# Weight units of a hybrid mixer and MoE kernel laid out so that each partition's 16 KB are contiguous in memory

## What is computed

```python
x_n = rms_norm(x, mix_norm_g); h = x_n @ w_in            # (1024, 9216)
a_val, a_gb, a_gc, h_glu, q, h_gate = split(h)
y_a = (a_gb * conv3(a_gc * a_val)) @ w_out_a
u   = silu(layer_norm(conv31(glu(h_glu + b_glu)) + conv_b_b)); y_b = u @ w_out_b + b_out_b
y_x = cross_attention(q, rms_norm(mem), w_kv) @ w_out_x   # 4 heads, 256 memory tokens
x   = x + (gate0 * y_a + gate1 * y_b + gate2 * y_x) @ w_o
z   = rms_norm(x, ffn_norm_g)                             # top-1 group of 4, top-2 of its 8 experts
for e in range(32):
    gate, up = split(z @ w_gate_up[e])                    # (1024, 1024)
    x += combine[:, e] * ((silu(gate) * up) @ w_down[e])  # (512, 1024)
return rms_norm(x, final_norm_g)
```

## Time and profile before

| what | value |
|---|---|
| median of 3 runs (lowest, highest) | 1006.33 us (1005.08, 1006.57) |
| profiled execution, own device time | not given on the page |
| profiled execution, span | 1004.3 us |
| data moved by DMA | 270.6 MB, mean 269 GB/s |
| packets of SyncE's queue | 116,688 |
| dense part, routing, expert loop | about 0 to 400, 400 to 440, 440 to 990 us |

### The profile page before, as it was taken

How to read it: one execution, slowest core, us unless ns; L and a number is a source line. 1 busy time by engine, 2 the same in 40 slices (tenths; PEclk the granted TensorE clock), 3 DMA queues, 4 the chain that set the end, 5 groups by cost and what they waited for, 6 DMA issues and landing times.

```text
span 1004.3 us, 17558 instructions
## 1 busy us (share of the span) xinstructions
PE 932.6 (93%) x6914; PEld 812.2 (81%) x6914; DVE 854.5 (85%) x812; ACT 668.9 (67%) x649; POOL 211.6 (21%) x178
## 2 busy tenths in 40 slices
PE   5999989899999999499999999999999999999996
PEld 5998989899899998377777777777777777777774
DVE  4369999998765666679999999999999999999996
ACT  5553434344544645468888888788888888888885
POOL 0149999960001100410000000000000000000000
PEclk9999999999999999799999999999999999999998
DMA  9944534355422595269999999999999999999931
GB/s 341 355 169 144 191 121 167 133 207 212 168 85 98 205 385 214 84 222 327 357 357 348 365 363 344 364 352 363 343 364 363 350 358 351 363 348 361 363 132 42
DMA packets 118592, 270.60 MB, mean 269 GB/s; under 512 B 3360, under 2 KB 5536, under 8 KB 118560
## 3 DMA queue, kind: packets, MB, share of 16 engines
q1 hardware_dynamic: 116688, 267.37, 73.5%
q10 hardware_dynamic: 1872, 2.79, 0.8%
HBM read 269.10 MB, written 1.05 MB: 269 GB/s over the span
## 4 chain that ended last, share of the span: by engine, by line
PE 54%; DVE 29%; ACT 9%; issue 5%; DMA 1%; ACTq 1%; POOL 0%; DVEq 0%; SPq 0%
PE ps L1342 18%; DVE lo L980 11%; PE ps L1167 6%; PE ps L1169 6%; PE ps L1168 6%; PE ps L1367 6%; ACT hi L637 5%; DVE conv L852 5%; PE ps L1331 5%; DVE lo_last L980 4%; DVE lo L765 4%; PE ps L1184 1%; PE ps L1183 1%; PE ps L1182 1%; ACT silu_sb L723 1%
## 5 line engine op out<-in xcount | busy, mean ns | idle before, releaser
L980 DVE TENSOR_TENSOR lo<-raw,hi 128x2048 fp32r<-128x2048 f32 x142 | 328.5, 2339 | 4.2 <-ACT hi L637 4.2
L637 ACT ACTIVATE hi<-raw 128x2048 fp32r<-128x2048 f32 x141 | 267.5, 1909 | 3.0 <-PE ps L1342 3.0
L765 DVE TENSOR_TENSOR lo<-raw,hi 128x2048 fp32r<-128x2048 f32 x62 | 149.0, 2405 | 32.0 <-ACT hi L450 30.7
L1167 PE MATMUL ps<-inA,hi 128*128 128x256 f32 x576 | 166.2, 288 | 9.5 <-DVE lo L765 8.4
L450 ACT ACTIVATE hi<-raw 128x2048 fp32r<-128x2048 f32 x63 | 120.4, 1913 | 75.6 <-PE ps L1169 48.9
L1169 PE MATMUL ps<-inA,lo 128*128 128x256 f32 x576 | 164.4, 285 | 0.0
L1168 PE MATMUL ps<-inA,hi 128*128 128x256 f32 x576 | 164.4, 285 | 0.0
L1342 PE MATMUL ps<-hi,xeT 128*128 128x512 f32 x384 | 154.6, 403 | 5.8 <-DVE lo L980 5.2
L1342 PE MATMUL ps<-lo,xeT 128*128 128x512 f32 x384 | 150.1, 391 | 0.0
L422 POOL TENSOR_TENSOR hT<-h_sb,hT 128x256 fp32r<-128x256 f32 x32 | 33.9, 1059 | 524.9 <-ACT hT L682 524.9
L1167 PEld LDWEIGHTS ps<-inA,hi 128*128 128x128 f32 x576 | 112.1, 195 | 11.8 <-DVE lo L765 11.8
(11 more groups left out here) (213 smaller groups left out, 1632.7 us busy)
## 6 DMA issues: line engine op xcount, KB each, us to landing
raw<-in_w_gate_up SPq DMA_DIRECT2D x64, 2048.0 KB, 7.8
raw<-in_w_down SPq DMA_DIRECT2D x32, 2048.0 KB, 7.8
raw<-in_w_in SPq DMA_DIRECT2D x17, 2048.0 KB, 8.1
raw<-in_w_kv SPq DMA_DIRECT2D x4, 2048.0 KB, 8.4
raw<-in_w_out_a SPq DMA_DIRECT2D x2, 2048.0 KB, 7.7
raw<-in_w_out_x SPq DMA_DIRECT2D x2, 2048.0 KB, 7.8
raw<-in_w_out_b SPq DMA_DIRECT2D x2, 2048.0 KB, 8.8
raw<-in_w_o SPq DMA_DIRECT2D x2, 2048.0 KB, 7.6
```

What stands on the lines that cost most here:

```text
L637: nc.scalar.activation(expert_half(hi, N0), raw_flat(slot, k % 2), ACT.Copy).then_inc(hi_made, 1)
L765: nc.vector.tensor_tensor(conv_half(lo, N), raw_half(slot, h, k_split), conv_half(hi, N).bitcast(f32), ALU.subtract).then_inc(lo_made, 1)
L980: nc.vector.tensor_tensor(expert_half(lo, N0), raw_flat(expert_slot(m), k % 2), expert_half(hi, N0).bitcast(f32), ALU.subtract).then_inc(l ...
L1167: mm(dst, w_hi[:, k, c * P:(c + 1) * P], acts[:, 0, k, :], start=(k == 0), stop=False)
```

## The change

The host builds two new arrays. `w_dense` holds the 30 dense units one after the other, `w_experts` gate, up and down of each expert; in both a unit is stored as 128 rows of 4,096 floats, row p being exactly what partition p of the slot holds. Loads keep their order, their slots, their waits and their sizes; their source is now a block of 2 MB without gaps. Unit 0 is still loaded in two parts, now the first and second 8 KB of each row. For units outside `K_SPLIT` the host also puts the 256 columns of half 0 ahead of those of half 1, so that a half is always 2,048 contiguous floats in SBUF, and `raw_half` loses its case with gaps: ScalarE's line 450 and VectorE's line 765 read contiguously. What hi and lo hold is the same.

```diff
-        def raw_half(slot, h, k_split):
-            flat = raw[:, slot, :]
-            if k_split:
-                return flat[:, h * HALF:(h + 1) * HALF].rearrange("p (a b) -> p a b", b=T)
-            return flat.rearrange("p (a b) -> p a b", b=2 * T)[:, :, h * T:(h + 1) * T]
+        def raw_half(slot, h):
+            return raw_flat(slot, h).rearrange("p (a b) -> p a b", b=T)
...
-                src = matrices[matrix][:, c0:c0 + 512].rearrange("(k p) n -> p k n", p=P)
-                dst = raw[:, slot, :].rearrange("p (k n) -> p k n", n=512)
+                src, dst = w_dense[u], raw[:, slot, :]
                 if u == 0:
-                    sp.dma_start(dst[:, :, 0:T], src[:, :, 0:T]).then_inc(first_loaded, 16)
-                    sp.dma_start(dst[:, :, T:2 * T], src[:, :, T:2 * T]).then_inc(raw_loaded[slot], 16)
+                    sp.dma_start(dst[:, 0:HALF], src[:, 0:HALF]).then_inc(first_loaded, 16)
+                    sp.dma_start(dst[:, HALF:UNIT], src[:, HALF:UNIT]).then_inc(raw_loaded[slot], 16)
                 else:
                     sp.dma_start(dst, src).then_inc(raw_loaded[slot], 16)
...
-            gate_up = w_gate_up.rearrange("(j u) (k p) n -> u p j k n", u=2, p=P)
-            down = w_down.rearrange("(j u) (k p) n -> u p j k n", u=2, p=P)
+            experts = w_experts.rearrange("(j u) m p n -> u m p j n", u=2)
...
-                src = gate_up[parity, :, bass.ds(j, 1), :, c * FF:(c + 1) * FF]
-                sp.dma_start(raw[:, slot, :].rearrange("p (a k n) -> p a k n", a=1, n=FF), src)\
+                sp.dma_start(raw[:, slot, :].rearrange("p (a n) -> p a n", a=1), experts[parity, c, :, bass.ds(j, 1), :])\
                     .then_inc(raw_loaded[slot], 16)
...
-                src = down[parity, :, bass.ds(j, 1), :, :]
-                sp.dma_start(raw[:, slot, :].rearrange("p (a k n) -> p a k n", a=1, n=D), src)\
+                sp.dma_start(raw[:, slot, :].rearrange("p (a n) -> p a n", a=1), experts[parity, 2, :, bass.ds(j, 1), :])\
                     .then_inc(raw_loaded[slot], 16)
...
+    def unit(name, matrix, c0):
+        w = np.asarray(matrices[matrix][0])[:, c0:c0 + 512].reshape(KT, P, 512)
+        if name in K_SPLIT:
+            return w.transpose(1, 0, 2).reshape(P, UNIT)
+        return w.reshape(KT, P, 2, T).transpose(1, 2, 0, 3).reshape(P, UNIT)
+
+    w_dense = np.stack([unit(*u) for u in UNITS])
+    gate_up = np.asarray(w_gate_up[0]).reshape(E, KT, P, 2, FF).transpose(0, 3, 2, 1, 4).reshape(E, 2, P, UNIT)
+    down = np.asarray(w_down[0]).reshape(E, 1, FF // P, P, D).transpose(0, 1, 3, 2, 4).reshape(E, 1, P, UNIT)
+    w_experts = np.concatenate([gate_up, down], axis=1)
```

More of the change, by code:

```diff
@@ L88, with hybrid_moe_kernel @@
 AX = mybir.AxisListType
[L91 to L94, removed]
+def hybrid_moe_kernel(nc, x, mem, w_dense, w_experts, w_route, cols, rows, b_route, consts, out):
     ctx = ExitStack()
@@ L280, in _ @@
             sp.dma_start(col[:, :], cols).then_inc(col_loaded, 16)
-            for u, (name, matrix, c0) in enumerate(UNITS):
+            for u in range(N_UNITS):
                 slot = raw_slot(u)[0]
@@ L441, in _, with make_hi @@
         def _(act):
-            def make_hi(N, slot, loaded, h, k_split):
+            def make_hi(N, slot, loaded, h):
                 if N == 0:
@@ L449, in make_hi @@
                     act.wait_ge(half_used, N - (CONV - 1))
-                return nc.scalar.activation(conv_half(hi, N), raw_half(slot, h, k_split), ACT.Copy)
+                return nc.scalar.activation(conv_half(hi, N), raw_half(slot, h), ACT.Copy)
             def dense_hi(N):
@@ L454, in dense_hi @@
                     slot, before_ = raw_slot(N // 2)
-                    make_hi(N, slot, 16 * (before_ + 1), N % 2, UNITS[N // 2][0] in K_SPLIT).then_inc(hi_made, 1)
+                    make_hi(N, slot, 16 * (before_ + 1), N % 2).then_inc(hi_made, 1)
                 else:
@@ L458, in dense_hi @@
                     slot = expert_slot(m)
-                    make_hi(N, slot, 16 * (RAW_BASE[slot] + 1 + m // RAW), N % 2, True).then_inc(hi_made, 1)
+                    make_hi(N, slot, 16 * (RAW_BASE[slot] + 1 + m // RAW), N % 2).then_inc(hi_made, 1)
             act.wait_ge(warm_ready, 1)
@@ L761, in link, with make_lo @@
                 dve.wait_ge(dve_chain, chain[0])
-            def make_lo(N, slot, h, k_split):
+            def make_lo(N, slot, h):
                 dve.wait_ge(hi_made, N + 1)
-                nc.vector.tensor_tensor(conv_half(lo, N), raw_half(slot, h, k_split), conv_half(hi, N).bitcast(f32),
+                nc.vector.tensor_tensor(conv_half(lo, N), raw_half(slot, h), conv_half(hi, N).bitcast(f32),
                                         ALU.subtract).then_inc(lo_made, 1)
@@ L769, in dense_lo @@
                 if N < DENSE:
-                    make_lo(N, raw_slot(N // 2)[0], N % 2, UNITS[N // 2][0] in K_SPLIT)
+                    make_lo(N, raw_slot(N // 2)[0], N % 2)
                 else:
-                    make_lo(N, expert_slot((N - DENSE) // 2), N % 2, True)
+                    make_lo(N, expert_slot((N - DENSE) // 2), N % 2)
             roots = [0]
@@ L1464 @@
     put_const("desc_e", np.arange(E, 0, -1))
+    matrices = {"w_in": w_in, "w_out_a": w_out_a, "w_out_b": w_out_b, "w_out_x": w_out_x, "w_kv": w_kv, "w_o": w_o}
+    def unit(name, matrix, c0):
[7 more added lines that the diff above has]
+    w_experts = np.concatenate([gate_up, down], axis=1)
     vectors = (mix_norm_g, mem_norm_g, b_gate, b_glu, conv_a_w, conv_b_w, conv_b_b, ln_b_g, ln_b_b, b_out_b, ffn_norm_g)
     arrays = {
-        "x": x[0], "mem": mem[0], "w_in": w_in[0], "w_out_a": w_out_a[0], "w_out_b": w_out_b[0],
-        "w_out_x": w_out_x[0], "w_kv": w_kv[0], "w_o": w_o[0], "w_gate_up": w_gate_up[0], "w_down": w_down[0],
+        "x": x[0], "mem": mem[0], "w_dense": w_dense, "w_experts": w_experts,
         "w_route": np.concatenate([w_group[0], w_router[0]], axis=1),
```

## The result

| | before | changed |
|---|---|---|
| median | 1006.17 us (4 runs) | 1014.51 us (4 runs, 1012.32 to 1016.83) |
| ratio | 1 | 1.0084, 95% interval 1.0068 to 1.0101 |
| profiled execution: span | 1004.3 us | 1014.8 us |
| profiled execution: own time | not given on the page | 1016.83 us, the slowest of the four |

I had forecast 1005.4 us and a range up to 1007.3. The kernel became 8.3 us slower, by the rival in which large packets hold up the small queue, and by more than that rival had said (1009.2).

The account below looks back on a forecast made before the run. It took PE and DVE work as the bound, with the loads hidden by slack. First half unit 0.2, stalled issue 0.64 and conversions 0.1 summed to 0.9 us saved: 1005.4 us, range 1002.6 to 1007.3.

Parts of the forecast that it names:

- the rival in which large packets hold up the small queue: At the start, ScalarE's queue alternates with SyncE's 16 KB packets; line 479's stall grows by 3.1 us, to 1009.2; chance 0.09.
- ScalarE's stalled issue: Line 479 near the start holds ScalarE 3.91 us through SyncE's backlog; with fewer packets the stall goes, gaining 0.64 us.
- The expert loop: More than half of the span, 17.65 us a step; loads take 5.6 us of transfer, hidden by slack: no gain or loss.
- the rival with slow packets: In the expert loop, 16 KB packets from 763 ns up make it wait; at 800 ns 27 us more, 1033; chance 0.06.
- the 5.5 that the prediction had set aside: Transfer of one load in the loop, some 5.5 us by the Trainium skill's fixed packet cost; 5.6 was taken instead.
- The first half unit: The first 1 MB load at the start lands 0.3 us earlier (0.13 to 0.44), worth 0.2 us.
- PE's gap: TensorE's wait at the start before half 1, beginning at 23.02 instead of 22.38: 0.64 us, all gained if ScalarE's stall shrinks.
- The conversions: ScalarE and VectorE read dense halves without gaps: 0.1 us gained, bounds 0 and 0.5.
- Mem and w_route have room: ScalarE's small loads are needed late, mem at 49 us and w_route near 398, so their later needs have room.

Follow-up runs that it names:

- the last table: Three kernels with w_route in 128 rows against the kernel before: new layout with 16 KB rows 0.9968, new layout with 2 KB rows 0.9982, old layout 0.9974.
- the kernel without the stall: The kernel before, old layout, with w_route loaded as 128 rows instead of 1,024: 1004.01 us, ratio 0.9977; in more rounds 1002.60 us, 0.9974.

## Why the prediction was wrong

- **The step that failed is ScalarE's stalled issue.** It says: "ScalarE's own queue holds only 272 + 1,040 + 144, fewer than passed without a stall; so I read its stall as the other queue's backlog." That took a limit found on SyncE's queue (2,640 packets pending) and applied it to another queue. SyncE's own issues did lose their stalls (0.45 to 0.48 us for the three that had taken 2.87 to 4.51), so the limit held for its queue. On ScalarE's it did not: with SyncE's packets down to 1,280 issued, 944 of them passed by 14.69 us and 336 pending in place of 2,650, the stall grew from 3.9 to 11.1 us, and it vanished when ScalarE's own packets were fewer or its third load moved. The term was put at -0.64 us and was +7.1, with 2.7 us of slow clock on top. The evidence against was in the text: ScalarE's two issues before 479 met the same backlog and took under 0.5 us.
- **The rival had the mechanism and half the price.** It multiplied by 5 turns, the packets done when the stall ended. The runs show that the number of turns grows with the packet, to 11 or 12 beside 16 KB, and the stall grew by 7.2 us and not 3.1. It also left out what an idle TensorE costs afterwards: after 9.4 us the clock was at 0.50 and the next matmuls ran at half pace. With both it would have read 1006.3 + 7.2 + 2.7 - 0.2 = 1016.0, by the profiled run (1016.8) and above the median. Its chance of 0.09 was too low, since a large packet beside a small queue was exactly what the change makes.
- **The expert loop: right in time, not quite in transfer.** 17.67 us a step, no wait for a load. The price of a 16 KB packet, forecast at 628 to 704 ns, was 698; the rival with slow packets (763 ns and more) didn't occur. But "from 2 to 4 KB a byte gets no cheaper" came from short windows of a queue that wasn't full. Over the whole run SyncE's packets took 738 us of the 16 engines' time before and 714 after (share times span on the pages), and a load of the loop took 5.55 us, nearer to the 5.5 that the prediction had set aside than to its 5.6. The slack hid it.
- **The first half unit: right in kind, low in size.** It landed 0.6 us earlier (7.11 us after its issue for 7.72), forecast 0.3 with 0.44 as the bound. Whether that shortens the run by itself is what the last table leaves undecided.
- **PE's gap: wrong in size.** Removing the stall from the kernel before is worth 2 us (0.9977, 0.9974), not 0.64. The 0.64 was read behind a half 0 that had run in part at the slow pace. In the first trace of the kernel without the stall TensorE runs at the fast pace from its first matmul at 14.88, reaches half 1 2.14 us earlier and has no slow stretch at 401 us; which share of the 2 us is the clock's can't be told from single traces.
- **The conversions: right within their bounds**, 1,913 ns on ScalarE and 2,405 ns on VectorE before and after; the reads with gaps had cost nothing.
- **Mem and w_route have room: right.** mem landed 15.9 us after its issue in place of 8.4, and nobody waited.

## What to carry to other kernels

Where queues take turns packet for packet, as here, larger packets in one slow the other: mem's passed at 67 a microsecond beside 2 KB packets and at 23 beside 16 KB. Before a layout change look for small many-row loads issued beside it, above all on an engine that also computes, where the issue itself can block. Give such small loads few rows, or put them on the queue that only issues, behind the first large loads. A large transfer that is early anyway gains nothing from being faster: in this kernel 121 of 127 weight loads can have rows of 2 or of 16 KB with no difference that was measured.

## What the runs showed of the hardware that was not expected

- Two queues with work shared the 16 engines one packet for one packet: 159 against 158 packets in 7 us, though one kind was 16 KB and the other 4 KB, 2.34 MB against 0.65.
- A third load issued from ScalarE blocked it for 3.9 to 11.1 us with 91 packets an engine in its queue, and for 6.4 us with 83 (rows counted with one more packet a load for its semaphore); two loads with 82 were taken in under a microsecond together, and three with 35 took 0.45 to 0.51 us each.
- In the new arrays the 267 MB of SyncE's queue took 761 us of the 16 engines' time with rows of 2 KB, 718 with 4 KB, 709 with 8 KB and 714 with 16 KB (709 to 711 in the two runs of the 16 KB kernel with w_route in 128 rows). So 2 KB rows cost 6 to 7% more than 8 or 16 KB ones, and from 8 KB on there was nothing to gain. The old layout, three quarters 2 KB and one quarter 4 KB rows, took 738, less than the two prices would give; so where the rows lie may count as well, and the share of each isn't shown. The short window of rows 9 hides the difference: 8 x 87.6 = 701 ns against 698.
